# Inverse square roots of head and latent sums: from a reciprocal on VectorE and a root on ScalarE to a logarithm and an exponential on ScalarE

## What is computed

```python
def l2_normalize(x, eps=1e-6):
    return x32 * lax.rsqrt(jnp.sum(x32 * x32, axis=-1, keepdims=True) + eps)
# rwkv7_mixer
kk = l2_normalize(heads(k * k_k))
o = (o - mean) * lax.rsqrt(var + RWKV_GN_EPS)   # var: mean over a head of (o - mean)^2
# gdn_mixer
q = l2_normalize(q); k = l2_normalize(k)
o = rms_norm(o, norm_g) * silu(z)
# mla_mixer
rms_norm(c_q, q_norm_g) @ w_uq; rms_norm(c_kv, kv_norm_g) @ w_ukv
```

## Time and profile before

| | us |
|---|---|
| median of 3 runs | 2294.9 |
| lowest and highest | 2294.73, 2297.84 |
| the profiled execution: device time | 2294.88 |
| its span, first to last instruction | 2293.1 |

### The profile page before, as it was taken

One profiled execution on the slowest core, in us unless ns is written; L12 is line 12 of the kernel. 1 busy time (PEld: TensorE's weight loads), 2 busy tenths in 40 slices (PEclk: granted clock), 3 DMA queues, 4 the chain that ended last, 5 costly groups with the idle time before them and its releaser, 6 DMA issues.

```text
span 2293.1 us, 34619 instructions
## 1 busy us (share of the span) xinstructions
PE 2129.2 (93%) x14488; PEld 1654.4 (72%) x14488; DVE 1241.2 (54%) x1930; ACT 720.8 (31%) x1100; POOL 740.5 (32%) x550
## 2 busy tenths in 40 slices
PE   5988898998999999999989888899989999999997
PEld 3777677766666788888868766777656668888886
DVE  6785765798654332222358766568966544222223
ACT  3421321332333342323243133123242433423322
POOL 1530321332212444444434012123222144444442
PEclk7999998998999999999989999989999999999998
DMA  4320200221121232332232001012212122332321
GB/s 158 103 71 3 67 29 30 78 81 57 45 94 51 83 117 93 95 98 92 92 103 92 26 28 59 30 46 77 67 48 92 44 78 92 95 99 92 101 93 65
DMA packets 52266, 170.03 MB, mean 74 GB/s; under 512 B 5648, under 2 KB 13968, under 8 KB 51600
## 3 DMA queue, kind: packets, MB, share of 16 engines
q1 hardware_dynamic: 50928, 162.75, 22.2%
q0 software_dynamic: 1184, 5.07, 0.6%
HBM read 160.45 MB, written 7.34 MB: 73 GB/s over the span
## 4 chain that ended last, share of the span: by engine, by line
PE 76%; DVE 20%; ACT 2%; issue 2%; DMA 1%; SPq 0%; DVEq 0%; ACTq 0%
PE bank_a L464 11%; PE bank_a L465 11%; PE bank_a L468 11%; PE bank_v L468 7%; PE bank_v L464 7%; PE bank_v L465 6%; PE bank_v L583 5%; PE bank_v L525 3%; DVE arena L1752 2%; DVE m L1750 2%; DVE arena L1325 2%; PE bank_v L699 2%; DVE s_z L1425 1%; PE bank_v L681 1%; DVE mg L1331 1%
## 5 line engine op out<-in xcount | busy, mean ns | idle before, releaser
L425 POOL TENSOR_TENSOR w_lo<-ring,w_hi 128x512 fp32r<-128x512 f32 x536 | 734.1, 1392 | 1383.1 <-ACT w_hi L1046 1383.0
L464 PE MATMUL bank_a<-h_hi,w_hi 128*128 128x512 f32 x1440 | 587.3, 408 | 7.8 <-DVE h_lo L1359 4.8
L465 PE MATMUL bank_a<-h_lo,w_hi 128*128 128x512 f32 x1440 | 566.3, 393 | 0.0
L468 PE MATMUL bank_a<-h_hi,w_lo 128*128 128x512 f32 x1440 | 356.5, 390 | 0.0
L1046 ACT ACTIVATE w_hi<-ring 128x1024 fp32r<-128x1024 f32 x268 | 281.7, 1051 | 234.9 <-DVE arena L1867 220.5
L464 PEld LDWEIGHTS bank_a<-h_hi,w_hi 128*128 128x128 f32 x1440 | 272.9, 190 | 88.7 <-issue 18.8
L465 PEld LDWEIGHTS bank_a<-h_lo,w_hi 128*128 128x128 f32 x1440 | 273.6, 190 | 63.9 <-issue 9.3
L468 PEld LDWEIGHTS bank_a<-h_hi,w_lo 128*128 128x128 f32 x1440 | 270.8, 188 | 57.1 <-POOL w_lo L425 0.6
L1325 DVE TENSOR_TENSOR sg<-bank_v,sg 128x512 f32<-128x512 f32 x112 | 77.5, 692 | 339.7 <-PE bank_v L468 256.9
L464 PE MATMUL bank_v<-parts,w_hi 128*128 128x512 f32 x640 | 254.4, 398 | 1.4 <-DVE parts L1838 1.4
L465 PE MATMUL bank_v<-parts,w_hi 128*128 128x512 f32 x640 | 253.4, 396 | 0.0
(11 more groups left out here) (277 smaller groups left out, 2450.3 us busy)
## 6 DMA issues: line engine op xcount, KB each, us to landing
ring<-in_w SPq DMA_DIRECT2D x268, 512.0 KB, 3.5
out_ring<-in_w SPq DMA_DIRECT2D x64, 128.0 KB, 3.5
x_dram<-arena SPq DMA_DIRECT2D x2, 2048.0 KB, 7.6
arena<-x_dram SPq DMA_DIRECT2D x2, 2048.0 KB, 7.9
arena<-in_x SPq DMA_DIRECT2D x2, 1024.0 KB, 8.7
arena<-tabs POOLq DMA_DIRECT2D x4, 512.0 KB, 3.9
out_x<-arena SPq DMA_DIRECT2D x2, 1024.0 KB, 4.3
par<-in_par POOLq DMA_DIRECT2D x2, 937.0 KB, 7.2
```

The costliest lines, as they stand in the source:

```text
L425: ins = nc.gpsimd.tensor_tensor(w_lo[:, g % SPLIT, ks, :], raw, w_hi[:, g % SPLIT, ks, :].bitcast(F32), ALU.subtract)
L464: mm(b[:], w_hi[:, s, k, :], hi[:, k, :], start=k == 0, stop=False)
L465: mm(b[:], w_hi[:, s, k, :], lo[:, k, :], start=False, stop=False)
L468: ins = mm(b[:], w_lo[:, s, k, :], hi[:, k, :], start=False, stop=k == KT - 1)
```

## The change

DVE's reads of the sums and its reciprocals go. The sums are made in pool a (pool v before), and ACT reads each bank with a logarithm, which scales the sum and adds epsilon from a constant column; an exponential of minus a half times the result follows over all tiles of the place. The three semaphore steps between the engines become two. In ACT's order the roots of the GDN's queries and keys move ahead of the first gates (they came after the decays' exponentials), the root of the GDN's output moves from behind ds unit 1 to ahead of its read, and RWKV's first root moves ahead of the low-rank results g.

```diff
+    parts += [("freq_d", fd[:, None]), ("freq_m", fm[:, None]),
+              ("eps", np.full((P, 1), EPS)), ("gn_eps", np.full((P, 1), GN_EPS))]
...
-            def block_sums(l, need, k, src, tiles, done):
+            def block_sums(l, need, k, src, tiles, done, pool="v"):
                 pe.wait_ge(S[need], at(l, need, k))
                 for i in range(tiles):
-                    b, reader, emptied = banks.next("v", done)
+                    b, reader, emptied = banks.next(pool, done)
                     pe.wait_ge(reader, emptied)
-                    mm(b[:], cst("blocks"), src[:, i, :], start=True, stop=True).then_inc(v_full, 1)
+                    mm(b[:], cst("blocks"), src[:, i, :], start=True, stop=True).then_inc(a_full if pool == "a" else v_full, 1)
...
-                block_sums(l, "r_sq", 1, R["tmp"], 2, "r_l2")
+                block_sums(l, "r_sq", 1, R["tmp"], 2, "r_l2", "a")
...
-                block_sums(l, "r_sq2", 1, R["sq"], 2, "r_gv")
-                block_sums(l, "g_sq", 1, G["sq"], 4, "g_l2")
+                block_sums(l, "r_sq2", 1, R["sq"], 2, "r_gv", "a")
+                block_sums(l, "g_sq", 1, G["sq"], 4, "g_l2", "a")
...
+            def inverse_roots(dst, scales, eps, sums, roots):
+                for i, scale in enumerate(scales):
+                    act.wait_ge(a_full, filled.next())
+                    b = filled.bank()
+                    act_fn(dst[:, i, :], b[:], ACT.Ln, scale=scale, bias=cst(eps)).then_inc(S[sums], 1)
+                act.wait_ge(S[sums], sums_done(sums, len(scales)))
+                act_fn(dst, dst, ACT.Exp, scale=-0.5).then_inc(S[roots], 1)
...
+                if l == 0:
+                    act.wait_ge(more_here, 16)
...
                 take_rw(4)
+                inverse_roots(R["tmp"], (1.0, 1.0), "eps", "r_l2", "r_l2s")
                 take_low_rank("g", None)
                 take_rw(5)
-                act.wait_ge(S["r_l2r"], at(l, "r_l2r", 1))
-                act_fn(R["tmp"], R["tmp"], ACT.Sqrt).then_inc(S["r_l2s"], 1)
...
                 act_fn(G["bh"], G["zi"], ACT.Sigmoid).then_inc(S["g_zs"], 1)
-                act.wait_ge(S["r_gr"], at(l, "r_gr", 1))
-                act_fn(R["sq"], R["sq"], ACT.Sqrt).then_inc(S["r_gs"], 1)
+                inverse_roots(R["sq"], (1.0 / C, 1.0 / C), "gn_eps", "r_gv", "r_gs")
+                inverse_roots(G["rs"], (1.0,) * 4, "eps", "g_l2", "g_l2s")
                 merge_sig(l)
...
-                act.wait_ge(S["g_l2r"], at(l, "g_l2r", 1))
-                act_fn(G["rs"], G["rs"], ACT.Sqrt).then_inc(S["g_l2s"], 1)
...
-                    if i == 2:
-                        act.wait_ge(S["g_gr"], at(l, "g_gr", 1))
-                        act_fn(G["sq2"], G["sq2"], ACT.Sqrt).then_inc(S["g_gs"], 1)
+                    if i == 1:
+                        inverse_roots(G["sq2"], (1.0 / C, 1.0 / C), "eps", "g_gv", "g_gs")
...
                 merge_sig(l)
-                act.wait_ge(S["m_rec"], at(l, "m_rec", 1))
-                act_fn(Mv["rs"], Mv["rs"], ACT.Sqrt).then_inc(S["m_rs"], 1)
+                inverse_roots(Mv["rs"], (1.0 / 256, 1.0 / 128), "eps", "m_nv", "m_rs")
                 merge_sig(l)
...
-                for f in range(2):
-                    dve.wait_ge(v_full, filled.next())
-                    b = filled.bank()
-                    v.tensor_scalar(R["sq"][:, f, :], b[:], 1.0 / C, GN_EPS, MUL, ADD).then_inc(S["r_gv"], 1)
-                    dve.wait_ge(S["r_gv"], reached("r_gv"))
-                v.reciprocal(R["sq"], R["sq"]).then_inc(S["r_gr"], 1)
-                dve.wait_ge(S["r_gr"], reached("r_gr"))
```

More of the change, by code:

```diff
@@ L133, in _constants @@
         fd[b + 8:b + 16] = inv_d
-    parts += [("freq_d", fd[:, None]), ("freq_m", fm[:, None])]
+    parts += [("freq_d", fd[:, None]), ("freq_m", fm[:, None]),
+              ("eps", np.full((P, 1), EPS)), ("gn_eps", np.full((P, 1), GN_EPS))]
     at, cols = 0, []
@@ L256, in build @@
             ("r_in", 8), ("r_zero", 1), ("r_mix", 8), ("r_act", 2), ("r_lora", 6), ("r_cum", 1), ("r_dec", 3),
-            ("r_ex", 1), ("r_sq", 1), ("r_l2", 2), ("r_l2r", 1), ("r_l2s", 1), ("r_bsq", 2), ("r_bon", 2), ("r_feat", 4),
+            ("r_ex", 1), ("r_sq", 1), ("r_l2", 2), ("r_l2s", 1), ("r_bsq", 2), ("r_bon", 2), ("r_feat", 4),
             ("r_tok", 8), ("r_mat", 8), ("r_x1", 2), ("r_ti", 2), ("r_y", 10), ("r_t", 8), ("r_x", 10),
             ("r_wt", 2), ("r_y1", 2), ("r_u", 2), ("r_ws", NC), ("r_s", NC), ("r_o", NC),
-            ("r_mean", 2), ("r_sq2", 1), ("r_gv", 2), ("r_gr", 1), ("r_gs", 1), ("r_out", 1),
+            ("r_mean", 2), ("r_sq2", 1), ("r_gv", 2), ("r_gs", 1), ("r_out", 1),
             ("g_in", 6), ("g_z", 2), ("g_conv", 6), ("g_sig", 6), ("g_sq", 1), ("g_l2", 4),
-            ("g_l2r", 1), ("g_l2s", 1), ("g_qk", 1), ("g_t1", 1), ("g_sp", 1), ("g_t2", 1), ("g_g", 2), ("g_feat", 6), ("g_gc", 1),
+            ("g_l2s", 1), ("g_qk", 1), ("g_t1", 1), ("g_sp", 1), ("g_t2", 1), ("g_g", 2), ("g_feat", 6), ("g_gc", 1),
             ("g_row", 2), ("g_d", 2), ("g_prep", 1),
@@ L265, in build @@
             ("g_wt", 2), ("g_u", 2), ("g_ws", NC), ("g_s", NC), ("g_o", NC),
-            ("g_sq2", 1), ("g_gv", 2), ("g_gr", 1), ("g_gs", 1), ("g_out", 1),
+            ("g_sq2", 1), ("g_gv", 2), ("g_gs", 1), ("g_out", 1),
             ("misc_in", 2), ("ab_in", 1),
@@ L269, in build @@
             ("d_ss", 16), ("d_p", 16), ("d_pn", 16), ("d_pt", 16), ("d_o", 16), ("d_kz", 2),
-            ("m_in", 2), ("m_sq", 1), ("m_nv", 2), ("m_rec", 1), ("m_rs", 1), ("m_c", 1), ("m_q", 4), ("m_k", 4), ("m_v", 2),
+            ("m_in", 2), ("m_sq", 1), ("m_nv", 2), ("m_rs", 1), ("m_c", 1), ("m_q", 4), ("m_k", 4), ("m_v", 2),
             ("m_rot", 4), ("m_kr", 4), ("m_krb", 1),
@@ L826, in _ @@
                     if i == 1:
-                        block_sums(l, "g_sq2", 1, G["sq2"], 2, "g_gv")
+                        block_sums(l, "g_sq2", 1, G["sq2"], 2, "g_gv", "a")
                     feat_group(("ds", i), l, h_hi, h_lo, "a", "d_in" if i < 8 else "d_vf")
@@ L871, in _ @@
                 pe.wait_ge(S["m_sq"], at(l, "m_sq", 1))
-                b, reader, emptied = banks.next("v", "m_nv")
+                b, reader, emptied = banks.next("a", "m_nv")
                 pe.wait_ge(reader, emptied)
@@ L875, in _ @@
                     ins = mm(b[:], cst("ones"), Mv["sq"][:, k, :], start=k == 0, stop=k == 1)
-                ins.then_inc(v_full, 1)
-                b, reader, emptied = banks.next("v", "m_nv")
+                ins.then_inc(a_full, 1)
+                b, reader, emptied = banks.next("a", "m_nv")
                 pe.wait_ge(reader, emptied)
-                mm(b[:], cst("ones"), Mv["sq"][:, 2, :], start=True, stop=True).then_inc(v_full, 1)
+                mm(b[:], cst("ones"), Mv["sq"][:, 2, :], start=True, stop=True).then_inc(a_full, 1)
                 merge(l, 3, 0, 2)
@@ L1080, in attention, with sums_done @@
                     fill(i)
+            def inverse_roots(dst, scales, eps, sums, roots):
[5 more added lines that the diff above has]
+                act_fn(dst, dst, ACT.Exp, scale=-0.5).then_inc(S[roots], 1)
+            sums_counts = {}
+            def sums_done(name, n):
+                sums_counts[name] = sums_counts.get(name, 0) + n
+                return sums_counts[name]
             split_next()
@@ L1644, in _ @@
                 dve.wait_ge(S["r_out"], reached("r_out"))
-                link(v.reciprocal(G["rs"][:, 2:4, :], G["rs"][:, 2:4, :]))
                 merge(l, True)
@@ L1675, in _ @@
                     dve.wait_ge(S["g_row"], reached("g_row"))
-                v.reciprocal(G["rs"][:, 0:2, :], G["rs"][:, 0:2, :]).then_inc(S["g_l2r"], 1)
-                dve.wait_ge(S["g_l2r"], reached("g_l2r"))
                 dve.wait_ge(S["g_l2s"], at(l, "g_l2s", 1))
@@ L1700, in _ @@
                 dve.wait_ge(S["g_sq2"], reached("g_sq2"))
[L1701 to L1707, removed]
                 dve.wait_ge(S["g_gs"], at(l, "g_gs", 1))
@@ L1797, in _ @@
                 merge(l)
[L1798 to L1807, removed]
                 dve.wait_ge(S["m_rs"], at(l, "m_rs", 1))
```

## The result

| us | before | after |
|---|---|---|
| median | 2294.9 | 2306.98 |
| lowest and highest (5 runs each) | 2292.82, 2297.84 | 2302.5, 2307.64 |
| the profiled execution: device time, span | 2294.88, 2293.1 | 2307.64, 2305.8 |

The ratio is 1.0047, 95% interval 1.0032 to 1.0061, or 10.8 us (7.3 to 14.0). The change alone makes the kernel slower: the 8.8 us forecast lie inside the interval, and the medians are 12.1 us apart (2303.7 was forecast, 2306.98 measured). The lines shift by one up to 1046, and by more behind (671 is now 672, 1660 is 1653); the logarithm is line 1088, the exponential 1090.

A forecast was written before the change was run, and what follows sets the result against it. TensorE, busy 93% of the span, was taken as the bound, so removed VectorE work gains 0; stalls of 2 x (1.1 + 3.3) = 8.8 us on 2294.9 give 2303.7 us (+0.38%), range 2297.5 to 2309.

The forecast's parts named there:

- The removed work: On VectorE, six reciprocals and twelve reads of sums a layer, 95.2 us in all, hidden at every site: gain 0.
- Two loads a call: On ScalarE, each call of inverse_roots has two table loads of 1.28 us, four loads more a layer.
- RWKV's L2: At RWKV's keys, low rank 1 on TensorE waits for the first logarithm to free its bank: 1.1 us a layer.
- Variance and the GDN's L2: The fourth GDN sum on TensorE waits for a bank until the first of four logarithms ends: 3.3 us a layer.
- The late sites: At the GDN's mean square and MLA's latents, no stall; the added loads fall into ScalarE's idle time: 0.
- The clock: Rival at the 3.3 us stall: the granted clock falls too, in both layers 3.4 us more, 2307.1 us; 29%.
- the alignment of DVE and GpSimd: Rival from line 1579 to the first inversion: slow VectorE instructions turn fast, 0.9 us each, 2290.2 or 2289.3 us; 6%.
- The shared table: Rival on ScalarE: logarithm and exponential share one table set, stalls 1.1 and 0.7 us, 2298.5 us; 7%.
- The stalls were not given back: Rival: the 3.3 us vanish in TensorE's wait for line 1660, 2297.1 us, or no bank is short, 2294.9; 9%.
- The doubled load: Rival on ScalarE: each table load costs twice, stalls 2.4 and 7.1 us, 2313.9 us; 2%.

The follow-up runs named there:

- keys_only: The kernel before with the change made only at RWKV's keys (RWKV's L2): 2298.52 us, ratio 1.0009.
- late_only: The kernel before with the change made only at the GDN's output and MLA's latents: 2293.64 us, ratio 0.9995.
- early decays: The decays' steps put ahead of VectorE's two merges: 2292.87 us on the kernel before, 2282.18 us on reordered.
- reordered: As grouped, and at RWKV's keys the low rank of g ahead of the sums on TensorE and ScalarE: 2299.12 us, ratio 1.0016.
- grouped: The changed kernel with the six logarithms of variance and the GDN's L2 in a row, both exponentials behind them: 2303.52 us, ratio 1.0042.

## Why the prediction was right

**The removed work, 95 us at no gain.** Right: 98.8 us of VectorE's busy time are gone and nothing of it shows in the time, and the reciprocals alone, cut, give a ratio of 1.0001.

**Two loads a call.** Right: ten calls, twenty loads, 1283 ns each, and 53 loads in the whole kernel for 45 before, the eight more of the forecast. The Trainium skill, "ScalarE: Activation LUTs", section on table sets, has one load for the pair; the trace of the kernel after disagrees as that of before did.

**RWKV's L2, 1.1 us.** Right: a wait of 1.1 us in each layer, the logarithm at 81.10 for the 81.24 forecast, and 2.1 us in keys_only. The forecast had it go on to the end. In the profile 0.9 to 1.0 us of it are gone again before the second site, in either layer, over a stretch where the clock was lower before (0.89 from 150 to 180 us, and 0.94 after).

**Variance and the GDN's L2, 3.3 us.** Right in place and cause. By the starts of matching matmuls the site takes 3.3 us in layer 1 and 6.1 in layer 2. The wait itself is 2.96 us in layer 2 and 1.60 in layer 1, where three slow sums filled the rest. With one load more it grows by 1.4 and 1.5 us.

**The late sites at 0.** Right for what was changed there: late_only has 0.9995.

**The clock.** The forecast's 8.8 us left it out, and the rival that gave 2307.1 put it in for both layers. The profile lies between. In layer 1 the fall cost nothing at this site. In layer 2 TensorE is 3.24 us late ahead of the sums (1362.54 for 1359.30) and 9.35 at line 798. These 6.1 us are the late start of the fourth sum (3.1), its own slowness (0.6) and that of the gate's first matmuls (2.4). The term that was too small is the second site's in layer 2, by 2.8 us.

**A term that is missing.** Between line 798 and the latents of layer 2 the delay grows from 9.35 to 12.75 us. The new wait of line 819, 2.6 us, is most of it. The prediction had "the alignment of DVE and GpSimd" as a rival that makes the kernel faster, on the supposition that VectorE's long instructions are those beside GpSimd's. The trace of the kernel before bears the supposition out: of 151 VectorE instructions on two 128x512 tiles in SBUF (TENSOR_TENSOR, arena<-arena), 22 took over 1.5 us, and each had GpSimd at work for at least 0.64 of its time; 124 took 0.69 us, and 5 of these had GpSimd beside them. But the kernel after has 29 long ones, not fewer: the alignment went the other way. That it is the cause of the wait fits the rows of line 1338 (1.49 us for 0.42) and 1760, and no experiment here moves it by itself.

**How much was luck.** The mechanism and the two sites are shown. The nearness of the sum is in part luck: in the profile layer 1 cost 2.8 us up to its latents and layer 2 another 9.9, for 4.4 and 4.4 forecast.

**The rivals.** The shared table falls with the twenty loads. The stalls were not given back at the merges: the wait at line 798 is 6.2 us as before. The doubled load falls with ScalarE's rows, where the next activation starts 0.01 us behind a load of 1.28. The faster case didn't come.

## What to carry to other kernels

Before moving work to an idle engine, ask whether the work lay on the path at all, and which small pool of buffers the new reader has to empty. Here 95 us of free VectorE work were paid for with two short stalls of TensorE behind three banks. Put activations of one table in a row, and count a load at each change unless the trace shows a shared one. Freed time is worth something only after dependent work has been moved into it: early decays gave 0.9994 in the kernel before (its two reciprocals made one) and 0.9946 in the changed one (reordered).

## What the runs showed of the hardware

- The granted clock fell to half after a wait of 2.05 us and within the short sums behind it in some profiles (0.64, 0.62 and 0.66 over 4 us in after, reordered and keys_only) and stayed at 1.00 in others (before, and grouped in layer 1). In before and keys_only the instructions at this place are the same. Behind the wait of 6.2 us it stood at 0.50.
- The mean clock of a run of the kernel before lies between 0.960 and 0.967, and the time goes with it by 1.2 us a thousandth (correlation -0.84 over 69 runs). Differences under 0.2% are better compared at one clock.
- A VectorE instruction on two 128x512 tiles in SBUF took 0.69 us, and 1.5 to 1.8 us in 22 cases, each with GpSimd at work beside it for at least 0.64 of the time; 5 of the 124 short ones had GpSimd beside them too (kernel before).
